# ScalarE's copy of transposed probabilities ahead of the exponential of a later task, and token tiles in mixed order

## The reference

```python
def masked_softmax(s, mask):
    s = jnp.where(mask, s.astype(jnp.float32), NEG)
    return jnp.where(mask, jax.nn.softmax(s, axis=-1), 0.0)
...
    s = jnp.einsum('bqghd,bqgksd->bqghks', q, k_g) * scale      # selected blocks
...
    o_slc = jnp.einsum('bqghks,bqgksd->bqghd', p.reshape(shp).astype(v_g.dtype), v_g)
    s = jnp.einsum('bqghd,bwgd->bqghw', q, kw) * scale          # window
...
    o_win = jnp.einsum('bqghw,bwgd->bqghd', p.astype(vw.dtype), vw)
    g = jax.nn.sigmoid(gates)
    return g[..., 0:1] * o_cmp + g[..., 1:2] * o_slc + g[..., 2:3] * o_win
```

## Time and profile before

| | us |
|---|---|
| median of 3 runs (1377.1 to 1379.44) | 1379.4 |
| the profiled execution | 1378.66 |
| its span | 1376.8 |
| TensorE busy (matmuls) | 1254.6 (91%) |
| VectorE busy | 829.9 (60%) |
| ScalarE busy | 301.7 (22%) |
| GpSimd busy | 355.8 (26%) |
| copies of bank 5 in the chain that ended last (L1164) | 1% of the span |
| exponentials in that chain (L1155) | 2% of the span |

### The profile page before, as it was taken

How to read it: one execution, slowest core, us unless ns; L and a number is a source line. 1 busy time by engine, 2 the same in 40 slices (tenths; PEclk the granted TensorE clock), 3 DMA queues, 4 the chain that set the end, 5 groups by cost and what they waited for, 6 DMA issues and landing times.

```text
span 1376.8 us, 20622 instructions
## 1 busy us (share of the span) xinstructions
PE 1254.6 (91%) x7761; PEld 1018.3 (74%) x7761; DVE 829.9 (60%) x1370; ACT 301.7 (22%) x831; POOL 355.8 (26%) x422
## 2 busy tenths in 40 slices
PE   6999899999998668889999999995999999999996
PEld 5878776668887445555678888784888888888885
DVE  6779332237888476776775545657565465467445
ACT  3463210020010355554410111014000000000012
POOL 5932324312220012222211111110111112413542
PEclk9899999999999889999999999996999999999998
DMA  9223445547677223433554222412113122132101
GB/s 253 64 92 119 146 111 173 149 164 262 238 243 257 82 78 116 127 101 116 168 230 122 77 76 91 170 62 76 62 62 122 61 78 106 62 111 73 62 0 62
DMA packets 122002, 166.15 MB, mean 121 GB/s; under 512 B 36448, under 2 KB 90400, under 8 KB 117552
## 3 DMA queue, kind: packets, MB, share of 16 engines
q1 hardware_dynamic: 103408, 104.72, 24.1%
q0 software_dynamic: 8080, 50.58, 10.3%
q10 hardware_dynamic: 10416, 9.54, 2.1%
HBM read 159.34 MB, written 13.84 MB: 126 GB/s over the span
## 4 chain that ended last, share of the span: by engine, by line
PE 79%; DVE 10%; ACT 6%; issue 3%; another core or an unknown queue 1%; DMA 0%; DVEq 0%; POOL 0%; ACTq 0%; PEldq 0%
PE PS L2274 43%; PE PS L1867 11%; PE PS L2038 9%; PE PS L1844 4%; PE PS L1993 2%; ACT R L1155 2%; DVE small L1656 2%; PE PS L2182 2%; PE PS L2150 2%; PE PS L2212 1%; DVE PS L1654 1%; ACT R L1164 1%; ACT KVU L1054 1%; PE PS L2017 1%
## 5 line engine op out<-in xcount | busy, mean ns | idle before, releaser
L1867 PE MATMUL PS<-hT,stream 128*128 128x260 f32 (+1 forms) x800 | 188.7, 397 | 8.0 <-ACT KVU L1056 4.1
L1867 PEld LDWEIGHTS PS<-hT,stream 128*128 128x128 f32 (+1 forms) x800 | 154.5, 195 | 40.1 <-issue 4.7
L2274 PE MATMUL PS<-R,stream 128*128 128x260 f32 x720 | 168.9, 383 | 2.4 <-PE PS L2274 2.4
L2274 PEld LDWEIGHTS PS<-R,stream 128*128 128x128 f32 x720 | 135.7, 190 | 25.8 <-issue 5.5
L2274 PE MATMUL PS<-R 128*128 128x260 f32 x576 | 130.8, 383 | 3.3 <-DVE R L1819 2.1
L2038 PE MATMUL PS<-R 128*128 128x256 f32 (+1 forms) x544 | 121.8, 383 | 5.2 <-DVE R L1497 2.4
L2274 PEld LDWEIGHTS PS<-R 128*128 128x128 f32 x576 | 109.3, 190 | 21.1 <-DVE R L1819 2.5
L2274 PE MATMUL PS<-R,QO 128*128 128x260 f32 x544 | 123.6, 383 | 1.4 <-DVE QO L1700 1.4
L1774 DVE TENSOR_TENSOR R<-PS,R 128x260 f32<-128x260 f32 x100 | 42.6, 426 | 126.1 <-PE PS L2274 125.3
L2038 PEld LDWEIGHTS PS<-R 128*128 128x128 f32 x544 | 102.0, 197 | 22.1 <-issue 6.1
L2274 PEld LDWEIGHTS PS<-R,QO 128*128 128x128 f32 x544 | 103.3, 190 | 17.6 <-DVE QO L1700 1.8
(11 more groups left out here) (420 smaller groups left out, 1938.4 us busy)
## 6 DMA issues: line engine op xcount, KB each, us to landing
stream<-in_cache_kv_slc SPq DMA_DIRECT2D x128, 128.0 KB
stream<-in_w_mlp_up SPq DMA_DIRECT2D x8, 2048.0 KB
stream<-in_w_mlp_down SPq DMA_DIRECT2D x8, 2048.0 KB
stream<-in_w_in SPq DMA_DIRECT2D x4, 2048.0 KB
stream<-in_state_kv_win SPq DMA_DIRECT2D x16, 512.0 KB
stream<-in_w_in SPq DMA_DIRECT2D x8, 1024.0 KB
out_kv_win_sample<-in_state_kv_win POOLq DMA_DIRECT2D x1, 8176.0 KB, 43.3
R<-in_cache_kv_slc SPq DMA_DIRECT2D x56, 128.0 KB
```

The source lines that it names most:

```text
L1867: ins = M(pair(u)[0:w, hf, 0:HALF], lhs[k], rhs[k][:, HALF * hf:HALF * hf + HALF], start=(k == 0), stop=(k == n - 1))
L2274: ins = M(product_of(w, i), lhs[:, k, :], rhs[:, k, :], start=(k == 0), stop=(k == nk - 1))
```

## The change

Two things. On ScalarE the copy of task n-2 (`at_a`) stands ahead of the exponential of task n. The exponential's own wait on `at_full` is dropped: it kept the exponential from overwriting `PP` before the transposes of n-2 had read it, and the copy in front of it waits for the same count. And `TASKS` is written in another order: the pairs (r = 0, 1) of a head come in four rounds of six, with the tiles 3, 0, 2, 3, 1, 2. All other loops read `TASKS`, so all engines follow.

```diff
-        TASKS = [(t, p, h, r, 2 if t < 2 else 1) for t in range(TT) for p in range(2)
-                 for h in range(0, HPG, 2 if t < 2 else 1) for r in range(2)]
+        HEADS = [[(t, p, h, 2 if t < 2 else 1) for p in range(2) for h in range(0, HPG, 2 if t < 2 else 1)]
+                 for t in range(TT)]
+        TASKS = []
+        for i in range(4):
+            for t, at in ((3, 2 * i), (0, i), (2, 2 * i), (3, 2 * i + 1), (1, i), (2, 2 * i + 1)):
+                t_, p, h, nx = HEADS[t][at]
+                TASKS += [(t, p, h, r, nx) for r in range(2)]
...
             for n in range(NTK + 3):
-                if n < NTK:
-                    t = TASKS[n][0]
-                    act.wait_ge(as_max, n + 1)
-                    if n >= 2:
-                        act.wait_ge(at_full, n - 1)
-                    for i, x, j, c0 in softmaxes(n):
...
-                    ins.then_inc(as_exp, 1)
                 if 2 <= n <= NTK + 1:
                     m = n - 2
...
                                          blocks(m, PS[:, 5, :], P * (t + 1)), ACT.Copy).then_inc(at_a, 1)
+                if n < NTK:
+                    t = TASKS[n][0]
+                    act.wait_ge(as_max, n + 1)
+                    for i, x, j, c0 in softmaxes(n):
...
+                    ins.then_inc(as_exp, 1)
```

More of the change, by code:

```diff
@@ L1147, in _ @@
             for n in range(NTK + 3):
-                if n < NTK:
-                    t = TASKS[n][0]
-                    act.wait_ge(as_max, n + 1)
-                    if n >= 2:
-                        act.wait_ge(at_full, n - 1)
-                    for i, x, j, c0 in softmaxes(n):
-                        k = 4 * (n % 2) + i
-                        ins = nc.scalar.activation(PP[:, n % 2, j, c0:c0 + P * (t + 1)], score_block(n, j, c0),
-                                                   ACT.Exp, bias=amx[:, k:k + 1], accum_out=asm[:, k:k + 1])
-                    ins.then_inc(as_exp, 1)
                 if 2 <= n <= NTK + 1:
@@ L1165, in _ @@
                                          blocks(m, PS[:, 5, :], P * (t + 1)), ACT.Copy).then_inc(at_a, 1)
+                if n < NTK:
+                    t = TASKS[n][0]
+                    act.wait_ge(as_max, n + 1)
+                    for i, x, j, c0 in softmaxes(n):
+                        k = 4 * (n % 2) + i
+                        ins = nc.scalar.activation(PP[:, n % 2, j, c0:c0 + P * (t + 1)], score_block(n, j, c0),
+                                                   ACT.Exp, bias=amx[:, k:k + 1], accum_out=asm[:, k:k + 1])
+                    ins.then_inc(as_exp, 1)
                 if n >= 3 and TASKS[n - 3][3] == 1:
```

## The result

The changed kernel took 1361.33 us, the median of 6 runs (1355.86 to 1362.88), against 1378.75 for the kernel before in as many: a ratio of 0.9878, 95% interval 0.9865 to 0.9890, or 17.4 us less. The profiled execution has a span of 1359.1 us in place of 1376.8, 17.7 less.

| | before | after | difference |
|---|---|---|---|
| ahead of prompt attention | 497.6 | 495.9 | -1.7 |
| prompt attention | 185.0 | 165.4 | -19.6 |
| behind it | 694.2 | 697.8 | +3.6 |

A forecast was written before the change was run, and what follows sets the result against it. Prompt attention was held bound by TensorE's 23.6 us idle, nearly all waiting for ScalarE's copy; 15.4 + 0.4 = 15.8 us off the 1379.4 us median gave 1363.6, stated as 1363.5, range 1356 to 1373.

The forecast's parts named there:

- Part A: In prompt attention, ScalarE's copy ahead of the exponential lets transposes start earlier: 15.4 us gained, bounds 9.8 and 22.8.
- The releasers named next: What the transposes would wait for once ScalarE's copy is early: TensorE's scores, GpSimd's scaling or VectorE's copy.
- the leftovers: Transposes' waits remaining per task after the moved copy: 0.17, 0.63, 0.75 us in tiles 2, 1, 0; 6.9 in all.
- The delayed exponential: On ScalarE, 24 exponentials with r = 0 come up to half a microsecond later behind the moved copy; counted as nothing.
- the first rival: Each r = 0 exponential comes later by a copy and transposes wait for GpSimd: 9.4 us lost, 1372.9 us; chance 0.12.
- Part B: Prompt attention's task pairs in mixed tile order move next to nothing: 0.4 us gained, bounds +5.5 and -3.1.
- The averaging of chain and cover: At tile borders, VectorE's chain and the TensorE work covering it each take about the two tiles' mean; 0.40 or 0.38 us left.
- The second rival: Mixed order exposes VectorE at 24 pair starts, 1.1 us each, 26 us in all: 1390 us; chance 0.04.
- The clock: TensorE's granted clock in prompt attention, 0.98 in the mean: up to 1.8 us won or lost, left out of the sum.
- The decode slabs and the weights: Page slabs have 42 us where two need 36, so nothing should wait; weights behind prompt attention move forward with it.
- Nothing comes out: Prompt attention gets shorter but the stage behind waits for its weights: 1379.4 us; chance 0.03.
- TensorE becomes the bound: All 22.8 us of waits on ScalarE's copy go and the clock stays up: 1356.6 us; chance 0.13.

The follow-up runs named there:

- the third comparison: Only ScalarE's copy moved, tasks in the old order, 1338.22 us (ratio 0.9877 to the kernel before), beside the whole change, 1340.45 us (0.9894).

## Why the prediction was right, point by point

The forecast was 1363.5 us in a range from 1356 to 1373, and 1361.3 came: 17.4 us less where 15.8 were forecast. The mechanism held; that the total came so close owes something to luck. In the profiles the stage gained 19.6 us in place of 15.8, 1.7 more came ahead of it, and 3.6 were given back behind it; neither of these was in the sum.

- **What bounds the stage** held: idle time of TensorE, nearly all of it behind ScalarE's copy. That time went from 22.8 us to none.
- **Part A, 15.4 us, is a little too large.** The idle time that the copy alone takes away is 14.3 us in one profile and 13.5 in three (23.6 to 10.1). The releasers named next were right in kind: VectorE's copy and GpSimd's scaling, with 8.4 to 9.0 us of waits in place of 6.9. In the third comparison they are 4.2, 2.3, 1.7 and 0.8 us in tiles 0, 1, 2 and 3, where the leftovers were 3.0, 2.5, 1.4 and none. So most of what was missed is one thing, GpSimd's scaling in tile 0.
- **The delayed exponential** was priced at nothing. Transposes wait for GpSimd's scaling 2.1 us in the whole change and 3.6 to 4.3 in the copy alone, where the first rival wanted 9.4. No run takes the delay by itself, so what part of the 1.2 us in tile 0 is due to it stays open.
- **Part B, 0.4 us, is mis-sized.** On top of the moved copy the mixed order takes 2.0 to 2.9 us off the stage (167.5 to 168.3 against 165.4 to 165.5). Of this 0.7 to 1.5 is idle time (9.4 or 10.1 against 8.6 or 8.7), and the rest busy time. Without the moved copy it takes nothing off the idle time (23.5 against 23.6 us). The averaging of chain and cover failed: with other neighbours the same six pairs take 4.7 us more. The Trainium skill's rule (Perfetto Trace Analysis, Optimization Strategy: interleaving regimes may gain) holds for the order of the change and not for the other one, which at 170.1 us is slower than no mixing; the 5.5 us that I worked out from the rule came in neither. The second rival, that mixed neighbours expose VectorE and make the kernel slower, was wrong for this order: waits on VectorE rose from 4.8 to 6.2 us and those on GpSimd fell from 3.6 to 2.1.
- **The clock** was left out of the sum, with up to 1.8 us either way. It was worth more: TensorE's busy time in the stage fell by 4.6 us, and by 3.6 with the order alone. It was wrong to expect busy time within 2 us of 161.8 and no change behind the stage. An estimate without the clock: a slow stretch of 3.4 us cost 1.7 us behind the stage, and the kernel before had two in the stage, so without them its stage would take 181.6 us. The copy alone (167.6) then brings 14.0, the order alone (181.3) 0.3, and both (165.4) 16.2 us, near the 15.8 of the sum, with part A too large and part B too small.
- **The decode slabs and the weights** held nothing up. No wait of TensorE in the stage or behind it names a transfer.
- **Nothing comes out** fell, and so did **TensorE becomes the bound**: 8.6 us of idle are left.
- Three slips of the working change nothing: eight times 0.38 is 3.0 and not 3.1, the transposes of tile 0 start at 503.99 and not at 503.98, and the 11.8 us for which TensorE waits on VectorE behind the stage are three waits, the longest of 9.2.

What stays open is which is faster in total, the whole change or the copy alone. By the stage it is the whole change, by 2.0 to 2.9 us. The totals of three comparisons say 3.0 us for the copy alone, 2.9 for the whole change, 2.2 for the copy alone. The slow stretches behind the stage move either by up to 3.6 us, and those ahead of it by up to 5.7; neither part was changed, and both kernels reach 694.3 to 694.4 us behind the stage. The runs bring out no version that beats the changed kernel beyond this doubt.

## What to carry to other kernels

Where an engine's list puts an operation whose input has been ready for long behind one that has yet to wait, swap them, if the one passed over waits for no later event than the one moved; take the gain as the distance to the next releaser of whoever was waiting, not as the whole wait. Look at what then stands behind the moved wait: the same move took 16.7 us off the stage on ScalarE and added 52.7 us on VectorE, where the next maximum came to stand behind it. Compare stage by stage, since stretches at the lower clock elsewhere can give or take several microseconds, and take more than three profiles before calling their place fixed. Read from the trace what added work costs: here it was 2.8 us and not the 1.6 that was meant.

## What the runs showed of the hardware

- Behind one and the same wait of 2.1 us, TensorE's clock fell to 1.2 GHz for 3.4 us in three of four profiles of the whole change, and stayed at 2.4 GHz in the fourth and in the kernel before. The three, which agreed within 0.2 us, had looked like a fixed place. The Trainium skill (TensorE: Matmul & The Clock Gate, What's actually happening) says that the monitor's phase runs free of the kernel and that the ramp varies from run to run; the fourth profile agrees.
- The same instructions behind the stage took 694.2 to 697.9 us, in steps of 1.5 to 1.8 us, by which of two places fell at 1.2 GHz; those ahead of it took 471.7 or 477.4 us on one chip, with 50.1 us of idle time in both.
- The mixed order alone, with 23.5 us of idle time unchanged, ran at a clock of 1.00 in the stage, where the kernel before had 0.98 (one profile each).
- The stage of prompt attention in the mixed order with the copy moved took 165.4 to 165.5 us in all five profiles, though what is ahead of it took from 471.7 to 495.9 us on different chips.
